# Attention mixing with the probabilities as weights, and the maxima's row sent through DRAM

## The reference, cut to what matters

```
def block(args):
    qn, qr = args
    s = (einsum('bqhd,bkhd->bhqk', qn, k_nope) + einsum('bqhd,bkd->bhqk', qr, k_rope)) * scale
    p = softmax(s, axis=-1)
    return einsum('bhqk,bkhd->bqhd', p, v)
```

## Time and profile before

| | |
|---|---|
| median of 3 runs | 3884.38 us |
| profiled execution | 3887.53 us, of which the profile's span is 3885.8 us |
| mean granted TensorE clock | 0.958 of full speed |
| PE (matrix products) busy | 3559.1 us (92%) |
| DVE (VectorE) busy | 2205.4 us (57%) |
| ACT (ScalarE) busy | 1532.3 us (39%) |
| attention phase | from 885.7 us (first load) to 1853.1 us (first load of the next phase) |
| the mixing products, 3 x 544 of 65 by 512 | 216.8, 213.9 and 214.8 us busy |
| the row's products, L1197 x320 in the trace | 42.2 us busy |
| the output's transposes, L1205 x160 | 16.4 us busy |

### The profile page before, as it was taken

One profiled execution on the slowest core, in us unless ns is written; L12 is line 12 of the kernel. 1 busy time (PEld: TensorE's weight loads), 2 busy tenths in 40 slices (PEclk: granted clock), 3 DMA queues, 4 the chain that ended last, 5 costly groups with the idle time before them and its releaser, 6 DMA issues. The chain is left out here.

```text
span 3885.8 us, 51505 instructions
## 1 busy us (share of the span) xinstructions
PE 3559.1 (92%) x19453; PEld 2991.9 (77%) x19453; DVE 2205.4 (57%) x3803; ACT 1532.3 (39%) x1959; POOL 218.2 (6%) x132
## 2 busy tenths in 40 slices
PE   5999969997999999999599739999999999999991
PEld 4888868875777777776477628999999999999991
DVE  4444457766777777776355454555555555545545
ACT  2111134444666666666223213433333333333335
POOL 0000000001000000000011100100000000000100
PEclk9999989998999999999899859999999999999995
DMA  2112145656211222200433124555555555555546
GB/s 105 60 59 74 53 156 202 217 212 140 53 20 39 55 53 53 53 8 5 144 135 135 76 87 142 162 168 169 158 176 157 157 172 163 167 167 157 165 127 241
DMA packets 314712, 470.46 MB, mean 121 GB/s; under 512 B 79073, under 2 KB 215009, under 8 KB 311905
## 3 DMA queue, kind: packets, MB, share of 16 engines
q1 hardware_dynamic: 302816, 426.94, 34.8%
q0 software_dynamic: 11776, 41.95, 5.1%
HBM read 352.83 MB, written 116.00 MB: 121 GB/s over the span
## 5 line engine op out<-in xcount | busy, mean ns | idle before, releaser
L63 PE MATMUL psum<-xeT_hi,w_hi 128*128 128x320 f32 x2048 | 635.2, 310 | 0.0
L64 PE MATMUL psum<-xeT_lo,w_hi 128*128 128x320 f32 x2048 | 633.5, 309 | 0.0
L65 PE MATMUL psum<-xeT_hi,w_lo 128*128 128x320 f32 x2048 | 633.5, 309 | 0.0
L1915 ACT ACTIVATE w_hi<-w_raw 128x2048 fp32r<-128x2048 f32 x192 | 358.6, 1908 | 295.5 <-PE psum L65 199.5
L1993 DVE TENSOR_TENSOR w_lo<-w_raw,w_hi 128x2048 fp32r<-128x2048 f32 x192 | 432.3, 2285 | 40.3 <-ACT w_hi L1915 40.3
L1228 ACT ACTIVATE p_hi<-psum 128x1024 fp32r<-128x1024 f32 x272 | 279.1, 1026 | 360.6 <-PE psum L65 360.6
L1275 DVE TENSOR_REDUCE mx<-psum 128x1 f32<-128x1024 f32 x256 | 312.9, 1224 | 168.9 <-PE psum L1152 168.9
L63 PEld LDWEIGHTS psum<-xeT_hi,w_hi 128*128 128x128 f32 x2048 | 385.1, 188 | 1.0
L64 PEld LDWEIGHTS psum<-xeT_lo,w_hi 128*128 128x128 f32 x2048 | 385.2, 188 | 0.6
L65 PEld LDWEIGHTS psum<-xeT_hi,w_lo 128*128 128x128 f32 x2048 | 385.2, 188 | 0.0
L1293 DVE TENSOR_TENSOR p_lo<-p_raw,p_hi 128x1024 fp32r<-128x1024 f32 x272 | 333.2, 1225 | 82.8 <-ACT p_raw L1230 79.5
(11 more groups left out here) (323 smaller groups left out, 6835.2 us busy)
## 6 DMA issues: line engine op xcount, KB each, us to landing
w_raw<-in_w_gate SPq DMA_DIRECT2D x64, 1024.0 KB, 6.2
w_raw<-in_w_up SPq DMA_DIRECT2D x64, 1024.0 KB, 9.4
w_raw<-in_w_down SPq DMA_DIRECT2D x64, 1024.0 KB, 5.2
rec<-rec SPq DMA_DIRECT2D x20, 768.0 KB, 3.6
recb<-rec SPq DMA_DIRECT2D x20, 768.0 KB, 5.1
xa<-in_x SPq DMA_DIRECT2D x20, 512.0 KB, 4.4
xb<-in_x SPq DMA_DIRECT2D x20, 512.0 KB, 6.0
xo<-in_x SPq DMA_DIRECT2D x20, 512.0 KB, 3.4
```

The source lines that it names most:

```text
L63: pe.matmul(out, a[0], b[0], start=first, stop=False)
L64: pe.matmul(out, a[0], b[1], start=False, stop=False)
L65: return pe.matmul(out, a[1], b[0], start=False, stop=last)
L1915: a.activation(w_hi[n % 4][:], raw[n % 4][:], ACT.Copy).then_inc(s["hi_made"], 1)
```

## The change

`mix` changes the roles. A 128 by 128 piece of `p_hi` or `p_lo` (128 keys, 128 queries) is the weights, and the values move. They stand in one tile of 130 columns, 64 of lo, 64 of hi and two of ones. For each of 4 groups of queries and 2 key tiles there are two products: `p_hi` with all 130 columns, and `p_lo` with the last 66. That is 16 products a slot in place of 6. The results stand with queries on partitions, two groups in bank 4 and two in bank 7. ScalarE copies both banks once a block into `mixed_in` (two copies of 128 by 260), and VectorE adds the two halves and divides. There is no `oT` and no transpose.

The maxima's row is no longer turned by the tensor engine. `unit` takes every fourth query of a block as its weights, so that `mx4`, read partition by partition, is the row in order. SP writes `mx4` to DRAM, waits for that to land and reads it back as one row into `qT_hi`; `score` of the block's first slot waits for the second landing. The sign is now in the key's constant row (-1).

```
+        def load_row(n):
+            g0, h, qb = starts[n]
+            dst = qT[h % 2][0][KQ:KQ + 1, 512 * qb:512 * (qb + 1)].bitcast(F32)
+            sp.wait_ge(s["mx4_made"], n + 1)
+            sp.dma_start(d["max_row"][n % 2].rearrange("(p q) -> p q", q=4), mx4[n % 2][:].bitcast(F32)
+                         ).then_inc(row_out[n % 2], 16)
+            sp.wait_ge(row_out[n % 2], 16 * (n // 2 + 1))
+            sp.dma_start(dst, d["max_row"][n % 2].unsqueeze(0)).then_inc(row_in[n % 2], 16)
         load(0)
         load(1)
-        for n, (g0, h, qb) in enumerate(starts):
-            if qb == 0 and 1 <= h < MH - 1:
+        for g in range(-AHEAD, TOTAL + 1):
+            if g in row_slot:
+                load_row(row_slot[g])
+            if g >= SLOTS and g % SLOTS == 2 and g // SLOTS < MH - 1:
+                h = g // SLOTS
                 sp.wait_ge(s["scored"], h * SLOTS)
                 sp.wait_ge(s["mixed"], h * SLOTS)
                 load(h + 1)
+            if g in out_slot:
+                store_out(out_slot[g])
 def unit(n):
-                qt, kb = 4 * qb + r // 2, 2 * (r % 2) + z
+                q, kb = r // 2, 2 * (r % 2) + z
+            fourth = slice(512 * qb + q, 512 * (qb + 1), 4)
-            ins = pe.matmul(ps[:, unit_bank(n) + z, :], qT[b][0][0:KQ, qt * P:(qt + 1) * P],
+            ins = pe.matmul(ps[:, unit_bank(n) + z, :], qT[b][0][0:KQ, fourth],
 def score(g):
             if j % 8 == 0:
-                pe.wait_ge(s["row_made"], block_no(g) + 1)
+                n = block_no(g)
+                pe.wait_ge(row_in[n % 2], 16 * (n // 2 + 1))
 def mix(g):
-            for z in range(2):
-                t = key_tile(j) + z
-                ins = mm3(pe, ps[0:MV + 1, 4, :], (vals[b][0][:, t, :], vals[b][1][:, t, :]),
-                          (p_hi[g % 4][:, z, :], p_lo[g % 4][:, z, :]), first and z == 0, last and z == 1)
+            for q in range(4):
+                at = VW * (q % 2)
+                cols = slice(q * P, (q + 1) * P)
+                for z in range(2):
+                    v_tile = vals[b][:, key_tile(j) + z, :]
+                    opens = first and z == 0 and q % 2 == 0
+                    closes = last and z == 1
+                    pe.matmul(ps[:, 4 + 3 * (q // 2), at:at + VW], p_hi[g % 4][:, z, cols], v_tile,
+                              start=opens, stop=False, skip_group_check=True)
+                    ins = pe.matmul(ps[:, 4 + 3 * (q // 2), at + MV:at + VW], p_lo[g % 4][:, z, cols],
+                                    v_tile[:, MV:VW], start=False, stop=closes, skip_group_check=True)
-        def turn_row(n):
-            for q in range(4):
-                ins = pe.matmul(ps[0:1, 7, q * P:(q + 1) * P], mx4[n % 2][:, q:q + 1], c.ident,
-                                start=True, stop=True)
-        def turn_out(n):
-            for q in range(4):
-                ins = pe.transpose(ps[:, 7, q * (MV + 1):(q + 1) * (MV + 1)], oT[:, q * P:(q + 1) * P],
-                                   c.const[0:MV + 1, C_ID:C_ID + MV + 1])
 ScalarE, take_out(n):
-            a.activation(oT[:], ps[0:MV + 1, 4, :], ACT.Copy).then_inc(s["oT_made"], 1)
+            for half in range(2):
+                ins = a.activation(mixed_in[n % 2][:, 2 * half:2 * half + 2, :].rearrange("p q e -> p (q e)"),
+                                   ps[:, 4 + 3 * half, 0:2 * VW], ACT.Copy)
 VectorE, take_out(n):
+            v.tensor_tensor(halves[:], src[:, :, 0:MV], src[:, :, MV:2 * MV], ALU.add)
```

More of the change, by code:

```diff
@@ L1062, in attention_phase @@
         kT = [(latents[0][:, b, :], latents[1][:, b, :]) for b in range(2)]
-        vals = [(sb(f"v_hi{b}", [P, NT, MV + 1], F32R), sb(f"v_lo{b}", [P, NT, MV + 1], F32R)) for b in range(2)]
+        VW = 2 * MV + 2
+        vals = [sb(f"v_lo_hi{b}", [P, NT, VW], F32R) for b in range(2)]
         p_raw = [sb(f"p_raw{b}", [P, 2, 512]) for b in range(2)]
@@ L1066, in attention_phase @@
         p_lo = [sb(f"p_lo{b}", [P, 2, 512], F32R) for b in range(4)]
-        oT = sb("oT", [MV + 1, 512])
+        mixed_in = [sb(f"mixed_in{b}", [P, 4, VW]) for b in range(2)]
+        halves = sb("halves", [P, 4, MV])
         o = [sb(f"o_sb{b}", [P, 4, MV]) for b in range(2)]
         mx, den = sb("mx", [P, 8]), sb("den", [P, 4])
-        mx4 = [sb(f"mx4_{b}", [P, 4]) for b in range(2)]
+        mx4 = [sb(f"mx4_{b}", [P, 4], F32R) for b in range(2)]
         hi_in = [c.sem(f"m_hi_in{b}") for b in range(2)]
@@ L1074, in attention_phase @@
         o_out = [c.sem(f"m_o_out{b}") for b in range(2)]
-        names = ("constant_rows scored hi_made raw_made lo_made mixed unit_scored unit_reduced mx4_made row_turned row_made "
-                 "oT_made out_turned den_made o_made").split()
+        names = ("constant_rows scored hi_made raw_made lo_made mixed unit_scored unit_reduced mx4_made "
+                 "taken halves_added den_made o_made").split()
         s = {n: c.sem("m_" + n) for n in names}
+        row_out = [c.sem(f"m_row_out{b}") for b in range(2)]
+        row_in = [c.sem(f"m_row_in{b}") for b in range(2)]
         NBH = NB * MH
@@ L1085, in attention_phase @@
         out_slot = {g0 + (8 if qb < 4 else 2): n for n, (g0, h, qb) in enumerate(starts)}
[L1086 to L1098, removed]
         def unit_bank(n):
@@ L1116, in load, with store_out @@
                     for w in range(2):
-                        sp.dma_start(vals[b][w][:, :, 0:MV].bitcast(F32), d["v"][w, :, :, MV * h:MV * (h + 1)].rearrange("t p e -> p t e")
+                        sp.dma_start(vals[b][:, :, MV * (1 - w):MV * (2 - w)].bitcast(F32), d["v"][w, :, :, MV * h:MV * (h + 1)].rearrange("t p e -> p t e")
                                      ).then_inc(v_in[b], 16)
+                def load_row(n):
[6 more added lines that the diff above has]
+                    sp.dma_start(dst, d["max_row"][n % 2].unsqueeze(0)).then_inc(row_in[n % 2], 16)
+                def store_out(n):
+                    g0, h, qb = starts[n]
+                    sp.wait_ge(s["o_made"], n + 1)
+                    sp.dma_start(d["o"][4 * qb:4 * qb + 4, :, h, :].rearrange("t p e -> p t e"), o[n % 2][:]
+                                 ).then_inc(o_out[n % 2], 16)
                 load(0)
                 load(1)
-                for n, (g0, h, qb) in enumerate(starts):
-                    if qb == 0 and 1 <= h < MH - 1:
+                for g in range(-AHEAD, TOTAL + 1):
[3 more added lines that the diff above has]
+                        h = g // SLOTS
                         sp.wait_ge(s["scored"], h * SLOTS)
@@ L1230, in exponentials @@
                     a.activation(p_raw[g % 2][:], src, ACT.Exp, scale=MSCALE).then_inc(s["raw_made"], 1)
[L1232 to L1236, removed]
                 def take_out(n):
@@ L1240, in take_out @@
                     a.wait_ge(s["mixed"], g0 + (8 if qb < 4 else 2))
-                    wait_from_one(a, s["out_turned"], n)
-                    a.activation(oT[:], ps[0:MV + 1, 4, :], ACT.Copy).then_inc(s["oT_made"], 1)
+                    wait_from_one(a, s["halves_added"], n - 1)
+                    wait_from_one(a, s["den_made"], n - 1)
+                    for half in range(2):
+                        ins = a.activation(mixed_in[n % 2][:, 2 * half:2 * half + 2, :].rearrange("p q e -> p (q e)"),
+                                           ps[:, 4 + 3 * half, 0:2 * VW], ACT.Copy)
+                    ins.then_inc(s["taken"], 1)
                 for g in range(-AHEAD, TOTAL + 1):
@@ L1255, in _ @@
                 for b in range(2):
-                    for part, value in ((kT[b][0][KQ:KQ + 1, :], 1.0), (kT[b][1][KQ:KQ + 1, :], 0.0),
-                                        (qT[b][1][KQ:KQ + 1, :], 0.0), (vals[b][0][:, :, MV:MV + 1], 1.0),
-                                        (vals[b][1][:, :, MV:MV + 1], 0.0)):
+                    for part, value in ((kT[b][0][KQ:KQ + 1, :], -1.0), (kT[b][1][KQ:KQ + 1, :], 0.0),
+                                        (qT[b][1][KQ:KQ + 1, :], 0.0), (vals[b][:, :, 2 * MV:VW], 1.0)):
                         wait_from_one(g, s["constant_rows"], n)
@@ L1296, in take_out @@
                 def take_out(n):
-                    v.wait_ge(s["out_turned"], n + 1)
-                    src = ps[:, 7, 0:4 * (MV + 1)].rearrange("p (q e) -> p q e", e=MV + 1)
+                    src = mixed_in[n % 2]
+                    v.wait_ge(s["taken"], n + 1)
                     wait_from_one(v, s["o_made"], n)
-                    v.reciprocal(den[:], src[:, :, MV]).then_inc(s["den_made"], 1)
+                    v.reciprocal(den[:], src[:, :, 2 * MV]).then_inc(s["den_made"], 1)
+                    v.tensor_tensor(halves[:], src[:, :, 0:MV], src[:, :, MV:2 * MV], ALU.add
+                                    ).then_inc(s["halves_added"], 1)
                     v.wait_ge(s["den_made"], n + 1)
+                    v.wait_ge(s["halves_added"], n + 1)
                     if n >= 2:
                         v.wait_ge(o_out[n % 2], 16 * (n // 2))
```

(2 more changed lines are left out.)

25 lines of the change are left out of this document (6 added, 19 removed).

## The result

The changed kernel takes 4712.43 us (median; 4711.96 to 4714.34) against 3886.09 us for the kernel before beside it: a ratio of 1.2127, 95% interval 1.2106 to 1.2148. The forecast was 4063 us with a range from 3930 to 4285. The direction is right; the time is far outside. 826 us were added where the forecast's sum had 179.

A forecast was written before the change was run, and what follows sets the result against it. PE's instructions were taken to bound each slot of the attention phase. 112 - 54 + 74 + 18 + 29 = +179 us gave a forecast of 4063 us; its own range was 4010 to 4125, the wider one 3930 to 4285.

The forecast's parts named there:

- Mixing price: Mixing in each slot: 16 products at 0.112 us, 1.79 us in place of 1.38, +112 us over 272 slots.
- C: Mixing products: weights load at the transposes' pace, slot 2.75 us, total 3853 us; chance 0.07.
- D: Mixing products: load and product come every 0.081 us, slot 3.15 us, total 3946 us; chance 0.04.
- B: Narrow float32r products at plain fp32's price: 4267 us, chance 0.14; with weights loaded twice 4471 us, chance 0.03.
- What goes: PE's products for the maxima's row (42 us) and the output's transposes (12 us) disappear: -54 us.
- The row behind the load: Row's DMAs queue behind a head's load: PE waits 12.3 us in heads 1 to 6, +74; first score +28.6 us.
- Rival A: SP's DMA queue: the row's DMAs land between those of the load, total 3942 us; chance 0.12.
- The clock: PE after each wait for the row: 6.4 us at half speed lose about 3 us, six times, +18 us.
- Six waits: Sign: PE waits about 12 us for the row's DMA six times, each 22 us after a load began.

The follow-up runs named there:

- The kernel with the rows ahead: Changed kernel with only SP's queue order altered: each head's load behind its second block's row, load(1) behind the first row; 3948.2 us, ratio 1.0163.

## Why the prediction was wrong

Its steps, one by one.

- **Mixing price, right.** 112 ns a product, a slot of 3.64 us; measured 0.22 us a pair and 3.65 us. The pair of a wide and a narrow one starts unevenly, and the sum is what holds. Rivals C and D, with shorter distances, are refuted by the 0.22 us a pair, and B, by which the moving columns count, by the experiments with more and with fewer columns.
- **What goes, right.** -54 us. The kernel with the rows ahead is at 3948.2 for 3885.8 + 112 - 54 + 5.5 = 3949.3.
- **The row behind the load, right in kind and nearly in size.** 10.8 us for 12.3 in head 1, and 27.8 for 28.6 at the start. Rival A is refuted. The write lands at 1102.0, 24.6 us after the load's first issue and not 25.8. Two ends of the forecast's range don't follow from its own figures: two DMAs of 3 us make a wait of 15.2 us, not 16, and 107 + 18 ns are 125 ns a product, not 121. Neither bears on the miss.
- **The clock, wrong, and with it the forecast.** The step that failed reads: "After such a rest the clock is the lower one ... 6.4 us at half speed lose about 3. Six times, +18 us." The fall was right. The 6.4 us of recovery were read from the earlier trace rows, where PE ran only products of 512 columns; they were then put behind a wait after which PE runs the new mixing. No row showed that mixing at the lower clock, and no bound was set for it. It was priced from one side only: the other end of this term is "not at all", which is 725 us for the first wait instead of 18 for six. Rival A was about the queue and the others about the price of a product; none asked whether the clock would return.
- **Six waits, one came.** A follow-up of the same error: at 6.83 us a slot, the five later rows are in time. Where the clock does return, all six came (slots of 13.9 to 14.6 us in the kernel with more columns moving), and with 4067.7 us that kernel stands where the forecast of 4063 stood. So close a match is partly luck: its waits are some 2 us shorter than forecast (12 us less in all), and its wider products make its slots 0.06 us longer (16 us more).

Shown by the runs: the wait is what starts the lower clock, the queue's order is what makes the wait, the narrow mixing holds either level, and wide products or more moving columns bring the higher one back. Not shown: what the chip counts to decide, and how short a wait may be without letting the clock fall. All the waits behind which it fell in this phase were of 10 to 13 us, and the one of 0.56 us let it stand. The Trainium skill's page "TensorE: Matmul & The Clock Gate", section "Why this matters for your kernels", says that activity gets the clock back and that gaps lose it; the second half agrees with this trace (the fall in the wait of 10.77 us), the first does not as it stands, since PE was busy for 1400 of 1400 us at 0.50. The measurement decides.

## What to carry to other kernels

A change that adds even one wait (here of 11 us) to the bounding engine can have two prices, the wait and the clock after it; the second has to be read from rows in which the engine does the work that will follow, not from any recovery in the trace. Short products whose weight loads set the pace look fully busy at either clock, so the busy share can't warn; look at the granted clock by stretch and at the distance of the same product in two places. And a small DMA that an engine waits for belongs ahead of a bulk load in a shared queue, or it takes the load's time (here the row's write landed 24.6 us after the load had begun, where ahead of it none of these waits was left).

## What the runs showed of the hardware that was not expected

- One kind of slot (six products of 512 columns for the scores, two for the maxima, 16 mixing products of 130 and 66) ran for 850 us at 1.00 and for 1400 us at 0.50, with PE busy throughout in both.
- The pace of float32r products with 128 weight columns goes with the granted clock: 0.22 us a pair at 1.00 and 0.42 at 0.50, and hardly with the moving columns between 66 and 256 (0.22 to 0.23 us a pair).
- More columns moving, none of them used, made a kernel 645 us faster (4712.4 to 4067.7 us), by the clock: its slots at 1.00 are 0.06 us longer, and it has five waits more.
